# A two-layer mixture-of-experts trunk: third expert matrices in four places, halves of the first two asked for early, experts written out

## The reference

```python
x = x + sgu_mixer(rmsnorm(x, a_norm), ...)                 # layer 0
x = x + hierarchical_moe(rmsnorm(x, m_norm[0]), ...)
k, v, cum = shared_kv(x, ...)
q, gate = jnp.split(h @ w_qg, 2, axis=-1)                  # layer 1
o = softmax(q k^T * scale + decay, masked) v
x = x + (o * jax.nn.sigmoid(gate)) @ w_out
x = x + hierarchical_moe(rmsnorm(x, m_norm[1]), ...)

def hierarchical_moe(h, ...):     # top-1 group of 4, then top-2 of its 8 experts
    hid = jax.nn.silu(xb @ w1[e]) * (xb @ w3[e])           # w1, w3: 32 x 1024 x 512
    return hid @ w2[e]                                     # w2: 32 x 512 x 1024
```

## Time and profile before

| | |
|---|---|
| median of the runs | 1584.84 us |
| the profiled execution | 1583.66 us, its span from first to last instruction 1581.9 us |
| TensorE busy | 1475.7 us, 93% |
| VectorE busy | 982.9 us, 62% |
| bytes moved | 461.12 MB, mean 291 GB/s |
| longest parts of the chain that ended last | TensorE 70%, DMA of expert matrices 23% |

### The profile page before, as it was taken

How to read it: one execution, slowest core, us unless ns; L and a number is a source line. 1 busy time by engine, 2 the same in 40 slices (tenths; PEclk the granted TensorE clock), 3 DMA queues, 4 the chain that set the end, 5 groups by cost and what they waited for, 6 DMA issues and landing times.

```text
span 1581.9 us, 45769 instructions
## 1 busy us (share of the span) xinstructions
PE 1475.7 (93%) x18889; PEld 1001.3 (63%) x18890; DVE 982.9 (62%) x2116; ACT 472.0 (30%) x796; POOL 25.8 (2%) x64
## 2 busy tenths in 40 slices
PE   7999999999999899988999999989899998998977
PEld 6788888755555556555778875458655554554544
DVE  5346642377777677675744457853777676675656
ACT  6442221412222222221543354533222121221211
POOL 3000000000000000000000000000000000000000
PEclk9999999999999999999999999999999999998999
DMA  6321322989999999999521322126899999999996
GB/s 216 123 106 54 107 94 73 385 332 428 429 428 429 428 428 429 429 428 428 199 99 61 121 80 81 40 65 255 345 389 428 428 429 428 428 429 427 430 429 294
DMA packets 55482, 461.12 MB, mean 291 GB/s; under 512 B 4496, under 2 KB 4640, under 8 KB 30848
## 3 DMA queue, kind: packets, MB, share of 16 engines
q1 hardware_dynamic: 51728, 453.00, 69.1%
q10 hardware_dynamic: 2192, 4.23, 0.8%
q0 software_dynamic: 1504, 3.07, 0.7%
HBM read 458.15 MB, written 2.13 MB: 291 GB/s over the span
## 4 chain that ended last, share of the span: by engine, by line
PE 70%; DMA 24%; DVE 4%; issue 2%; SPq 0%; ACT 0%; DVEq 0%; ACTq 0%
DMA EB<-in_m_w 23%; PE ps L1472 15%; PE ps L1311 10%; PE ps L1313 10%; PE ps L1312 10%; PE ps L1461 6%; PE ps L1482 6%; PE ps L1444 4%; PE ps L1687 2%; PE ps L1722 1%; PE ps L1741 1%; PE ps L1756 1%; PE ps L1574 1%; PE ps L1307 1%; PE ps L1373 1%
## 5 line engine op out<-in xcount | busy, mean ns | idle before, releaser
L1472 PE MATMUL ps<-EB,SCR 128*32 128x256 f32 x6016 | 366.7, 399 | 67.5 <-DMA EB<-in_m_w 53.6
L1472 PEld LDWEIGHTS ps<-EB,SCR 128*32 128x32 f32 x6016 | 196.4, 115 | 230.0 <-issue 102.2
L989 DVE TENSOR_TENSOR X<-X,ps 128x1024 f32 x188 | 221.1, 1217 | 30.0 <-PE ps L1444 30.0
L1313 PE MATMUL ps<-EB_r 128*128 128x512 f32 x512 | 200.2, 391 | 0.0
L1461 PE MATMUL ps<-H,SCR 128*32 128x256 f32 x3072 | 185.7, 382 | 0.0
L1482 PE MATMUL ps<-EB,SCR 128*32 128x256 f32 x3008 | 179.7, 379 | 0.0
L664 ACT ACTIVATE SCR_r<-ps,SCR 128x256 f32 x94 | 44.5, 473 | 448.1 <-PE ps L1482 448.1
L980 DVE TENSOR_TENSOR SCR<-SCR,ps 128x128 f32<-128x128 f32 x94 | 36.9, 393 | 209.3 <-ACT SCR L661 209.3
L1482 PEld LDWEIGHTS ps<-EB,SCR 128*32 128x32 f32 x3008 | 97.8, 110 | 64.7
L1312 PE MATMUL ps<-EB_r 128*128 128x512 f32 x352 | 137.7, 391 | 0.0
L1461 PEld LDWEIGHTS ps<-H,SCR 128*32 128x32 f32 x3072 | 90.0, 109 | 62.2
(11 more groups left out here) (277 smaller groups left out, 1661.3 us busy)
## 6 DMA issues: line engine op xcount, KB each, us to landing
EB<-in_m_w SPq DMA_DIRECT2D x192, 2048.0 KB, 26.7
EB<-in_a_w_in SPq DMA_DIRECT2D x7, 2048.0 KB, 8.2
EB<-in_a_w_out SPq DMA_DIRECT2D x4, 2048.0 KB, 7.9
EB<-in_kv_w SPq DMA_DIRECT2D x4, 2048.0 KB, 13.6
EB<-in_b_w_qg SPq DMA_DIRECT2D x4, 2048.0 KB, 7.9
EB<-in_b_w_out SPq DMA_DIRECT2D x2, 2048.0 KB, 9.5
X<-in_x SPq DMA_DIRECT2D x4, 512.0 KB, 7.0
EB<-in_a_w_in SPq DMA_DIRECT2D x4, 512.0 KB, 9.8
```

The lines of the kernel that those rows point to most:

```text
L989: add = v.tensor_tensor(X_t, X_t, moved[1][:, :, t, :], ALU.add)
L1313: return mm(o, left[1], right[0], start=False, stop=stop)
L1472: last = mm(ps[0][g * CAP:(g + 1) * CAP, 0:2 * P].rearrange("p (w n) -> p w n", w=2), xT[:, k, :], w13_sb[s][:, :, k, g * P:(g + 1) * P], ...
```

## The change

SBUF gets a tile WX; the third matrices go round four places (in EB1, EB2, EB0 and WX) and no longer three, so four of them can be asked for ahead. Four experts instead of three have the places of their numbers, and the other 28 are ranked with a step of 9 modulo 28: rank 0 stands at place 12, then 21, 30, 11, 20, 29, 10, 19, 28, 9, 18, 27, 8, 17, 26, 7 and so on. w1 and w3 are loaded in halves of their rows: the first halves once the expert three places back has finished half of its last first products (`up_half`), the second halves at `up`; then, at `down`, w2 of the expert one place further on. The round loop over three experts is gone on TensorE and SP: all 32 bodies are written out. The second gate tile is split into high and low parts, and gates 4 to 7 are split products. The split of the first output tile (`T_WO`) moves from units 18 to 21 to units 20, 22, 26 and 30, and its high part to the keys' place and WX. In the last units more of `attend_out` is done ahead.

```diff
+NW2 = 4
+        WX, WX_r = sb_split("WX", [P, KD * COL])
-        w2_sb = [EB[s][:, 2 * TILE:3 * TILE].rearrange("p (c n) -> p c n", c=KE) for s in range(NBUF)]
+        w2_sb = [at.rearrange("p (c n) -> p c n", c=KE)
+                 for at in [EB[s][:, 2 * TILE:3 * TILE] for s in (1, 2, 0)] + [WX[:, :]]]
...
-            def load_later_expert(l, e, s):
-                ended = sp.value_load(n0_i[0:1, bass.ds(e - (NBUF - 1), 1)], min_val=1, max_val=MAX_ITEMS)
-                expert = sp.value_load(place_i[0:1, bass.ds(e, 1)], min_val=NBUF, max_val=NE - 1)
-                sp.wait_ge(m["up"], ended)
-                sp.dma_start(w1_sb[s], w1e).then_inc(m["w13"][s], 16)
-                sp.dma_start(w3_sb[s], w3e).then_inc(m["w13"][s], 16)
-                sp.wait_ge(m["down"], ended)
-                sp.dma_start(w2_sb[s], w2e).then_inc(m["w2"][s], 16)
+            def load_first_two(l, e, expert, ended):
+                m, s = moe[l], slot(e)
+                for released, half in (("up_half", slice(0, KD // 2)), ("up", slice(KD // 2, KD))):
+                    sp.wait_ge(m[released], ended)
+                    for w, to in ((m_w1, w1_sb), (m_w3, w3_sb)):
+                        sp.dma_start(to[s][:, half, :], w[l][bass.ds(expert, 1), :, :]
+                                     .rearrange("a (p k) n -> p (a k) n", k=KD)[:, half, :]).then_inc(m["w13"][s], 16)
...
+                for e in range(NBUF, NE):
+                    ended = sp.value_load(n0_i[0:1, e - NBUF + 1:e - NBUF + 2], min_val=1, max_val=MAX_ITEMS)
+                    load_first_two(l, e, expert, ended)
+                    if e < NE - 1:
+                        expert = sp.value_load(place_i[0:1, e + 1:e + 2], min_val=NW2, max_val=NE - 1)
+                    if e < NE - 2:
+                        sp.wait_ge(m["down"], ended)
+                        load_third(l, e + 1, expert)
+                sp.wait_ge(m["down"], ended)
+                load_third(l, NE - 1, expert)
...
-                then(v.tensor_scalar(stride[0:NE, :], order[0:NE, :], -8.0, 224.0, ALU.mult, ALU.add))
+                then(v.tensor_scalar(stride[0:NE, :], order[0:NE, :], -9.0, 243.0, ALU.mult, ALU.add))
-                then(v.scalar_tensor_tensor(order[0:NE, :], order[0:NE, :], 8.0, place_base[0:NE, :], ALU.mult, ALU.add))
-                then(v.scalar_tensor_tensor(place[0:NE, :], place[0:NE, :], 29.0, order[0:NE, :], ALU.mult, ALU.add))
+                then(v.scalar_tensor_tensor(order[0:NE, :], order[0:NE, :], 9.0, place_base[0:NE, :], ALU.mult, ALU.add))
+                then(v.scalar_tensor_tensor(place[0:NE, :], place[0:NE, :], 28.0, order[0:NE, :], ALU.mult, ALU.add))
...
-                q = u - (PAIRS // 2 * NT + 3)
+                q = u - (2 * NT + 2)
                 if 0 <= q < 4:
+                    split_tile(T_G + 1, q, q + 1)
+                if u - 1 in WO_UNITS:
+                    q = WO_UNITS.index(u - 1)
                     split_tile(T_WO, q, q + 1)
...
+                            if k == KD // 2 - 1:
+                                last.then_inc(m["up_half"], 1)
                         last.then_inc(m["up"], 1)
...
-                with pe.Fori(0, (NE - 2) // NBUF) as r:
-                    ended = start_of(r * NBUF + 1)
-                    for s in range(NBUF):
-                        first, ended = ended, end_of(r * NBUF + s + 1)
-                        expert(slot(s + 1), r + (s + 1) // NBUF + 1, first, ended)
+                ended = start_of(1)
+                for e in range(1, NE - 1):
+                    first, ended = ended, end_of(e)
+                    expert(e, first, ended)
                 total = pe.value_load(n0_i[0:1, NE:NE + 1], min_val=NE, max_val=MAX_ITEMS)
                 keep_busy(0, 12, CW)
-                expert(slot(NE - 1), (NE - 1) // NBUF + 1, start_of(NE - 1), total)
+                expert(NE - 1, ended, total)
...
-            gate(0, 0, KD)
+            gate(0, 0, 5)
             turn_heads(15)
+            gate(0, 5, KD)
...
-                if u >= n_units:
-                    attend_out(0, 1, (0, 2, 5)[u - n_units], (2, 5, 7)[u - n_units])
+                    attend_out(0, 1, 0, 4)
+                if u == n_units + 1:
+                    attend_out(0, 1, 4, PAIRS - 1)
+                    attend_out(0, 2, 0, 2)
+                if u == n_units + 2:
+                    attend_out(0, 2, 2, PAIRS - 1)
```

More of the change, by code:

```diff
@@ L368, in attend_bank @@
         def attend_bank(g):
-            return ps[g % 2 if g else 7][:, :]
+            return ps[(7, 1, 0, 2, 7, 1, 0, 7)[g]][:, :]
         def slot(e):
@@ L420, in moe_loads @@
                 sp.wait_ge(m["tables"], 2)
-                with sp.Fori(1, NE // NBUF) as r:
-                    for s in range(NBUF):
-                        load_later_expert(l, r * NBUF + s, slot(s))
-                for e in range(NE // NBUF * NBUF, NE):
-                    load_later_expert(l, e, slot(e))
+                expert = NBUF
+                for e in range(NBUF, NE):
[8 more added lines that the diff above has]
+                load_third(l, NE - 1, expert)
             for t in range(NT):
@@ L626, in split_tile @@
             def split_tile(i, q0=0, q1=4):
-                split_hi(i % 2, i // 2 + i % 2, q0, q1, weight_gain(i))
+                scale = weight_gain(i)
+                act.wait_ge(tile_loaded[i % 2], 16 * (i // 2 + i % 2))
+                for q in range(q0, q1):
+                    if scale is None:
+                        last = a.activation(tile_hi(i, 2 * q, 2 * q + 2), ring[i % 2][:, 2 * q:2 * q + 2, :], ACT.Copy)
+                    else:
+                        for k in range(2 * q, 2 * q + 2):
+                            last = a.activation(tile_hi(i, k, k + 1)[:, 0, :], ring[i % 2][:, k, :], ACT.Copy,
+                                                scale=scale[:, k:k + 1])
+                    last.then_inc(w_hi, 1)
             def moe_act(l, ready):
@@ L854, in split_tile @@
             def split_tile(i, q0=0, q1=4):
-                split_lo(i % 2, split_no(i), q0, q1, weight_gain(i))
+                scale, j = weight_gain(i), i % 2
+                for q in range(q0, q1):
+                    dve.wait_ge(w_hi, 4 * i + q + 1)
+                    if scale is None:
+                        last = v.tensor_tensor(ring_lo[j][:, 2 * q:2 * q + 2, :], ring[j][:, 2 * q:2 * q + 2, :],
+                                               tile_hi(i, 2 * q, 2 * q + 2).bitcast(F32), ALU.subtract)
+                    else:
+                        for k in range(2 * q, 2 * q + 2):
+                            last = v.scalar_tensor_tensor(ring_lo[j][:, k, :], ring[j][:, k, :], scale[:, k:k + 1],
+                                                          tile_hi(i, k, k + 1)[:, 0, :].bitcast(F32), ALU.mult,
+                                                          ALU.subtract)
+                    last.then_inc(w_lo, 1)
             def bc(ap, n):
@@ L1463, in gather, with expert @@
                     last.then_inc(m["gath"], 1)
-                def expert(s, loads, r0, r1):
+                def expert(e, r0, r1):
+                    s = slot(e)
                     with pe.Fori(r0, r1) as n:
-                        pe.wait_ge(m["w13"][s], 32 * loads)
+                        pe.wait_ge(m["w13"][s], 32 + 64 * (e // NBUF))
                         pe.wait_ge(m["xT"], n + 1)
@@ L1699, in attend_out @@
                 if c0 == 0:
-                    pe.wait_ge(*((x_attn, g - 1) if g >= 2 else (s_max, 2 * (PAIRS * NT - 1)) if g else (g_scaled, PAIRS)))
+                    free = ((g_scaled, PAIRS), (s_max, 2 * (PAIRS * NT - 1)), (s_max, 2 * (PAIRS * NT - 1)),
+                            (s_max, 2 * PAIRS * NT), (x_attn, 1), (x_attn, 2), (x_attn, 3), (x_attn, 5))[g]
+                    pe.wait_ge(*free)
                 for c in range(c0, c1):
-                    if n == 0 and t == 0:
+                    if n == 0:
                         pe.wait_ge(o_gated, c + 1)
@@ L1758, in _ @@
                         last.then_inc(pt_tr, 1)
-            for t in range(2):
-                attend_out(0, t, PAIRS - 1, PAIRS)
-            for g in range(2, 2 * NT):
-                attend_out(g // NT, g % NT, 0, PAIRS)
+            for t in range(NT):
+                attend_out(0, t, PAIRS - 1 if t < NT - 1 else 0, PAIRS)
+            for t in range(NT):
+                attend_out(1, t, 0, PAIRS)
             router_end(1)
```

131 lines of the change are left out of this document (61 added, 70 removed).

## The result

The changed kernel takes 1621.72 us (median of 4 runs, 1620.98 to 1623.01); the kernel before, run beside it, takes 1584.55 us (1583.51 to 1587.21). The ratio is 1.0235, with a 95% interval of 1.0222 to 1.0248: 37 us slower. Forecast were 1614 us with a range of 1595 to 1628.

The account below looks back on a forecast made before the run. Expert-matrix loads at full DMA (427 to 428 GB/s) were taken to bound both expert stages. Layer 0 +16.9, layer 1 +15.0 and attention -2.6 sum to +29.3 us on 1583.66: forecast 1614 us, range 1595 to 1628.

Parts of the forecast that it names:

- The last group: Large experts right ahead of place 31: eight items, 66.6 us, in layer 0; six items, 50.0 us, in layer 1.
- the slow first product: First product at place 27, after TensorE has waited some 6 us: 5.35 us against 3.66, so 1.7 us more.
- the stalls at fetches: TensorE stalling when instructions are fetched: 0.5 us taken for a layer's last group.
- the fillers: Twelve products ahead of place 31 in each layer: 2.9 us, no longer covered by a wait for matrices.
- When w3 of place 27 comes: Layer 0's load ahead of the last group: tile 71 after the restart, at 696.3 us before halves and fetches are added.
- fetches, 2.4 us: 36 more instruction fetches on the DMA engines from 24 or 25 more bodies: 2.4 us a layer, bounds 0 and 4.8.
- Halves: w1 and w3 loaded as half tiles: 0.07 us a tile, 3.4 us in layer 0, 3.5 in layer 1; below, nothing.
- Attention: Split gates -3.8 us (by busy times -4.8), VectorE waits 0, output quarters +1.1 and +1.2, fills -0.4 and -0.7: -2.6.
- TensorE did not keep up: Rival for both layers' ends: TensorE keeps up, loads set both ends, -16 us, 1569 us; 8%.
- halves and fetches were not free: Rival: late ends, but halves and fetches cost nothing, +16.7 us, 1601.5 us; part of the forecast's 80%.
- the round loops' ends: Rival: 14 loop jumps were on the path; 13.6 us come off, 1571 us without the late ends; 1%.
- the dear-fetch rival: Rival: fetches stall TensorE at every block in the last groups and fall unevenly on DMA engines, +7.9 + 4.8, 1627 us; 8%.

Follow-up runs that it names:

- both variants late: Changed kernel with w1 and w3 asked for only after the predecessor's last up product: as whole tiles 1616.05 us, still in halves 1622.74 us.

## Why the prediction was right, and where it was off

The sum was +29.3 us on the profiled execution; the span grew by 36.9. The direction, the places and the mechanism held, and the two largest terms to 0.5 us:

- **The last group.** From place 27 to place 31: 704.73 to 776.05 is 71.3 us, forecast 1.7 + 66.6 + 0.5 + 2.9 = 71.7. Layer 1: 54.6 against 55.0. Inside, an item takes 8.30 us, the slow first product 2.0 instead of 1.7, the stalls at fetches nothing instead of 0.5, the fillers 2.9. That the order does it is shown from both sides: moved by two it gives back 26.5 us in the expert parts, and put into the kernel before it takes 19.4.
- **When w3 of place 27 comes.** Forecast 702.1 us, measured 704.73; in layer 1, counted from the layer's start, 392.8 and 396.1. This is the step that was mis-sized: fetches, 2.4 us, "if they go round all" engines. Their own time is right: with the 1.8 us by which a product follows its bytes in the kernel before, the terms put the bytes at 700.3 and 391.0 us, and they landed at 700.0 and 391.1. But the product came 4.7 and 4.9 us behind them, 2.9 and 3.1 more than before, and 3.0 more in the kernel before written out; the likely reason is that the fetches don't go round evenly. The text had this as the upper bound, 4.8 us for a layer; with 2.4 for their own time the whole is 5.3 to 5.5, above it. What the Trainium skill (Runtime: NRT & Kernel Launch, Instruction fetch mechanics) says, that fetching ahead hides the code, holds for TensorE here, whose first products wait 0.8 us in all for nothing but issue; the price is paid by the transfers beside it. (By the recorded terms the forecast without fetches would be 5.7 us lower, not 5.8.)
- **Halves.** Forecast 3.4 and 3.5 us for the rate; with both variants late, 3.9 us in layer 0. The early start was forecast at 1.8 us and is worth 1.7 and 2.7.
- **Attention.** Forecast -2.6, measured +0.2. This was off for two reasons of opposite sign. With half clock taken off as above the part is 3.3 to 4.9 us shorter. TensorE is busy 14.4 to 14.8 us in four units instead of 15.6 to 15.9, so the gates give about what the bound by busy times said (4.8). The waits for VectorE came where they were expected: 1.42 us twice in place of one of 1.09, and 4.27 where "above 4" was said. The two waits of 1.52 and 1.20 us are gone, and one of 1.62 us has come (shown below the list), released by VectorE's unit 11, where the low part stands ahead of the gate's scaling; with two waits of 0.3 us behind it that is about -0.5 where the term was 0. Then 13.6 us of half clock against 3.4 before take back up to 5.1 us. No term stood for that.
- **The rivals.** TensorE did not keep up; halves and fetches were not free; the round loops' ends were not on the path of the kernel before. Of the dear-fetch rival the later tiles came true (that the engines are uneven is inferred), the stalls of TensorE did not.

TensorE's wait for the gate's scaling:

```profile
993.96 0.50 PE L1339 MATMUL ps<-H_r,EB_r 128*128 128x512 f32 x1 [1.62 <-DVE EB L1262]
```

The remainder: 3.1 and 3.3 us for the start of the last group, 2.8 for attention, less 0.4 twice in the last groups, 0.4 ahead of the experts and 0.4 at the end, make the 7.6 us.

What stays open is why TensorE falls to half clock in one profile and not in the next: some 294 to 298 us behind the start of place 31 in eleven of the twelve kernels, some 11 to 13 us behind it in four. The two profiles of the changed kernel show that it can repeat; no run shows what sets it off.

## What to carry to other kernels

When loads and TensorE take turns as the bound, the order of uneven work matters most at the end: work that is left when the last load has been waited for hides behind nothing, so put the light items there and count them. Work that only keeps an engine warm, and ends of loops, cost nothing in front of a wait and their full time without one. Writing a loop out next to full DMA queues is not free; here rolling it up again was worth 1.9 us in one layer and 5.5 in the other. Where the granted clock differs between two profiles, compare them part by part before you believe a difference of a few microseconds in the whole.

## What was not expected of the hardware

- Fetches of instructions share the DMA engines with the data: some 38 fetches of 16 KB beside full queues made a layer's tiles 5.5 us later: 2.4 by their own time and 3.0 more that only kernels with such fetches show, most likely the lag of the engine that got most of them.
- Half as large transfers (1 MB instead of 2, rows of 8 KB instead of 16) moved 422 GB/s against 426, at full queues and with written out code in both.
- Stretches of 3.4 or 6.8 us at half clock came at the same places between the layers in both profiled executions of one kernel, while the profiles of twelve kernels have 0 to 13.6 us of them in that part, up to 6.8 us of time.
